# Expert biases: one row per quadrant of partitions and a VectorE shuffle in place of a broadcasting transfer

## The reference, cut to what matters

```python
    def expert_block(args):
        e, x_b = args
        gu = x_b @ w_gu[e] + b_gu[e]
        gate = jnp.minimum(gu[..., ::2], SWIGLU_LIMIT)
        up = jnp.clip(gu[..., 1::2], -SWIGLU_LIMIT, SWIGLU_LIMIT)
        return ((up + 1.0) * (gate * jax.nn.sigmoid(SWIGLU_ALPHA * gate))) @ w_dn[e] + b_dn[e]
```

## Time and profile before

| what | value |
|---|---|
| median of 3 runs | 3250.05 us (3247.81 to 3250.87) |
| the profiled execution's own time | 3250.61 us |
| its span, first to last instruction | 3248.8 us |
| mean granted TensorE clock | 0.910 of full speed |
| loop of 47 turns, about | from 1314 to 2548 us of the span |
| bytes moved by DMA | 569.55 MB |
| expert weight transfers called, skipped ones included | 576, of 1024 KB |
| bias transfers called, skipped ones included | 96, of 256 KB |

### The profile page before, as it was taken

The page is one execution under the profiler, slowest core; times in us unless marked ns, Lnnn a source line. Parts: engine busy times, 40 slices in busy tenths (PEclk is TensorE's granted clock), DMA queues, the critical chain, the costliest instruction groups (busy, mean ns, idle before and its releaser), DMA issues. The chain is left out here.

```text
span 3248.8 us, 51694 instructions
## 1 busy us (share of the span) xinstructions
PE 2634.1 (81%) x19262; PEld 1295.7 (40%) x19262; DVE 966.2 (30%) x2193; ACT 758.9 (23%) x1718; POOL 364.4 (11%) x339
## 2 busy tenths in 40 slices
PE   6778686856789993889888988898889589778999
PEld 2445363635464442323332323333333244355444
DVE  1263636363246425111111111111111321354012
ACT  2123332333050002222221212222222211254100
POOL 0030302130060000000000000000000200144000
PEclk8888787877899996899999999999999789887999
DMA  5100000000317314699999999499969612001112
GB/s 196 54 25 22 6 22 6 22 2 3 115 47 278 120 52 185 259 400 368 364 369 383 363 401 365 163 368 400 373 265 370 240 67 78 28 1 53 52 52 78
DMA packets 118951, 569.55 MB, mean 175 GB/s; under 512 B 13809, under 2 KB 17393, under 8 KB 67217
## 3 DMA queue, kind: packets, MB, share of 16 engines
q1 hardware_dynamic: 97184, 510.21, 40.2%
q10 hardware_dynamic: 15472, 36.16, 3.5%
q0 software_dynamic: 6144, 20.98, 1.8%
HBM read 760.50 MB, written 16.52 MB: 239 GB/s over the span
## 5 line engine op out<-in xcount | busy, mean ns | idle before, releaser
L1350 PE MATMUL moe_gu_ps<-expert_w,xgT 128*64 128x512 f32 x3008 | 683.1, 597 | 92.6 <-PEq L1315 92.6
L1350 PEld LDWEIGHTS moe_gu_ps<-expert_w,xgT 128*64 128x64 f32 x3008 | 245.4, 137 | 522.1 <-issue 522.1
L1376 PE MATMUL moe_down_ps<-expert_w,actT 128*64 128x512 f32 x1504 | 347.2, 598 | 67.4 <-PEq L1315 67.4
L1435 DVE TENSOR_TENSOR biased<-moe_gu_ps,b_gu 128x512 f32<-128x512 f32 x94 | 65.0, 692 | 936.9 <-DVEq L1315 936.9
L1376 PEld LDWEIGHTS moe_down_ps<-expert_w,actT 128*64 128x64 f32 x1504 | 114.4, 136 | 239.8 <-issue 239.8
L1397 ACT ACT_TABLE_LOAD x47 | 60.3, 1283 | 425.3 <-ACTq L1315 425.3
L1856 PE MATMUL ahead_ps<-hT,x 128*128 128x256 f32 (+1 forms) x288 | 127.6, 541 | 23.6 <-PEq L57 23.6
L1330 POOL COPY tokens<-token_of 128x1 uint32 x47 | 8.5, 182 | 1126.6 <-POOLq L1315 1126.6
L1279 ACT ACTIVATE xgT<-moe_xg_ps,ffn_shift,ffn_gain 128x64 f32<-128x64 f32 x384 | 119.0, 424 | 42.2 <-PE moe_xg_ps L1273 42.2
L1401 ACT COPY actT<-moe_act_ps 128x256 f32<-128x256 f32 x94 | 35.0, 372 | 399.9 <-ACTq L1315 399.9
L386 PE MATMUL b2p_ps<-b_w,b_hT 128*128 128x512 f32 (+1 forms) x320 | 119.4, 535 | 1.8 <-PEq L57 1.8
(11 more groups left out here) (684 smaller groups left out, 3685.0 us busy)
## 6 DMA issues: line engine op xcount, KB each, us to landing
expert_w<-in_w_experts SPq DMA_DIRECT2D x576, 1024.0 KB
late_w<-in_w_late SPq DMA_DIRECT2D x12, 2048.0 KB, 8.5
b_gu<-in_b_experts ACTq DMA_DIRECT2D x96, 256.0 KB
b_w<-in_w_in SPq DMA_DIRECT2D x10, 2048.0 KB, 7.6
ada_w<-in_w_ada SPq DMA_DIRECT2D x6, 2048.0 KB, 13.0
slot_rows<-yb ACTq DMA_DIRECT2D x94, 128.0 KB, 6.1
mix_w<-in_w_in_tok SPq DMA_DIRECT2D x5, 2048.0 KB, 9.9
x<-in_w_rkv SPq DMA_DIRECT2D x5, 1536.0 KB, 7.3
```

The lines of the kernel that those rows point to most:

```text
L1350: last = nc.tensor.matmul(ps_gu[SLOTS * j:SLOTS * j + SLOTS, half, :], xgT[:, k, :], w[:, i, at:at + 512], start=(k == 0), stop=(k == KD - 1),
L1376: last = nc.tensor.matmul(ps_dn[SLOTS * j:SLOTS * j + SLOTS, :], actT[:, half, q, SLOTS * a:SLOTS * a + SLOTS], w[:, i, at:at + 512], star ...
L1435: step(nc.vector.tensor_tensor(biased[:, :], ps_gu[:, half, :], b_gu[:, half, :], ALU.add))
```

## The change

A second buffer `b_rows` (128 partitions x 1024) is set to zero once. Each of the two bias transfers now writes one row of 4 KB into only two partitions (0 and 32 for row 0, 64 and 96 for row 1), the first partition of each group of 32. At the head of every turn VectorE waits for the bias, copies `b_rows` to `b_gu` with a shuffle in which all 32 partitions of a group take the group's first, and frees `b_rows`. The wait and the signal that stood in the two halves are gone.

```diff
+        b_rows = sb("b_rows", [P, D])
...
         def load_bias(act, expert, **when):
             for j in range(2):
-                act.dma_start(b_gu[SLOTS * j:SLOTS * j + SLOTS].rearrange("p h n -> p (h n)"),
-                              d["b_experts"][expert, j].unsqueeze(0).to_broadcast([SLOTS, D]), **when) \
+                act.dma_start(b_rows[SLOTS * j:SLOTS * j + SLOTS:32, :],
+                              d["b_experts"][expert, j].unsqueeze(0).to_broadcast([2, D]), **when) \
                     .then_inc(bias_here, 16)
...
+                nc.vector.memset(b_rows[:, :], 0.0).then_inc(s["rows_set"], 1)
...
             def _(act):
+                act.wait_ge(s["rows_set"], 1)
                 load_bias(act, 0)
...
                 with dve.Fori(0, turns):
+                    takes(dve, bias_here, 32)
+                    step(nc.vector.stream_shuffle(b_gu[:, :, :].rearrange("p h n -> p (h n)"), b_rows[:, :], [0] * 32))
+                    nc.vector.sem_inc(s["bias_free"], 1)
                     for half in range(2):
                         takes(dve, s["gu_made"])
-                        if half == 0:
-                            takes(dve, bias_here, 32)
                         step(nc.vector.tensor_tensor(biased[:, :], ps_gu[:, half, :], b_gu[:, half, :], ALU.add))
                         nc.vector.sem_inc(gu_read, 1)
-                        if half == 1:
-                            nc.vector.sem_inc(s["bias_free"], 1)
```

More of the change, by code:

```diff
@@ L1283, in modulate @@
             last.then_inc(xgT_made, 1)
-        with stage(nc, "moe_start", "tokens", "xg_turned", "set", pool_dma=(gathered,)) as (s, block):
+        with stage(nc, "moe_start", "tokens", "xg_turned", "set", "rows_set", pool_dma=(gathered,)) as (s, block):
             @block.vector
```

## The result

The changed kernel takes 3159.43 us in the median of 4 runs (3156.38 to 3165.14), against 3250.46 for the kernel before beside it. The ratio is 0.9718, with a 95% interval from 0.9697 to 0.9740: 91 us faster.

A forecast was written before the change was run, and what follows sets the result against it. The prediction took weight transfers in stretched groups of the expert loop's turns as the bound. 29 loads x 2.35 us = 68 us off 3250.6, other parts costing nothing, gave 3182 us, range 3168 to 3203.

The forecast's parts named there:

- eleven groups of turns: In the expert loop: 4 groups of three turns and 7 of four, where transfers run without pause; 29 loads inside.
- Saved per load: 2.78 - 0.43 = 2.35 us: In the expert loop: old bias transfer's cost less the new one's, counted for 29 loads, 68 us.
- What the new transfer costs: Per load in the expert loop: four 4 KB packets, two on the engine waited for, 0.43 us; bounds 0 and 0.86.
- long groups: Expert loop: 7 groups of four turns with two one-block experts, 108.79 us each, 15.2 above four unstalled turns; three loads each.
- What the old one costs: Per load in the expert loop: weights missing from five 6 us windows, 1.19 MB, 2.78 us (2.67 to 2.90).
- Short groups: Expert loop: 4 groups of three turns, two loads each; saving 4.7 of 5.3 us of stretch, so not cut off.
- the gather before the loop: Before the loop: shares engines with 0.52 MB less, could gain up to 1 us; left out of the sum.
- Price by bytes: In the expert loop, neighbours' slowing has another cause (mixing queues) and stays: only 35 us saved, 3215 us; chance 0.08.
- Two loaded engines: In the expert loop, many pieces fall on one or two engines, chunks wait: 17 or 114 us slower; chance 0.03.
- 13 packets' worth on one engine: Expert loop: the load on one engine, 2.78 / 0.21, from which the new transfer would make the kernel slower.
- The shuffle waits: VectorE's shuffle: rows landing over 13.4 us plus about 3 after the call; at 20 us, 112 slower; chance 0.02.
- the other signs: Loop: 2.5 MB weights per 6 us; groups 71 and 102 us; PE waits 60 us less; ScalarE queue 16 MB lighter.

The follow-up runs named there:

- kernel 3: Changed kernel without bias transfers in the loop, every expert given the first expert's bias, shuffle kept: 3159.47 us, 46 turns in 1121.93 us.
- experiment 12: Changed kernel with 16 KB instead of 4 KB for each of the four partitions, still two calls a turn: 3224.20 us, 46 turns in 1182.56 us.
- experiment 2: Changed kernel without the shuffle, VectorE adding b_rows itself, wait and signal where they were before the change: 3163.86 us.
- experiment 11: The changed kernel again, unaltered: 3161.09 us, 46 turns in 1126.01 us.
- kernel 9: Changed kernel with the shuffle made seven times in a row in each turn: 3160.92 us, 46 turns in 1125.18 us.
- kernel 1: Changed kernel with each bias transfer again covering all 64 partitions of b_rows, shuffle and earlier signal kept: 3247.72 us, ratio to before 1.0001.
- kernel 4: Kernel before, each partition reading its own 4 KB from the expert's weights instead of 64 partitions reading one row: 3249.54 us, ratio 1.0010.
- kernel 5: Kernel before, each of the two bias transfers writing every second of all 128 partitions instead of a block of 64: 3196.39 us, ratio 0.9832.
- kernel 6: Kernel before, one transfer over all 128 partitions read from the expert's weights, instead of two over 64 each: 3199.93 us, ratio 0.9864.
- experiment 10: Changed kernel with the shuffle made fourteen times in a row in each turn: 3468.16 us, 46 turns in 1422.03 us.
- kernel 8: Changed kernel with each two-partition transfer made four times, to four different sets of partitions: 3223.35 us, 46 turns in 1187.22 us.

## Why the prediction was wrong in size

The mechanism was right at every step: the loop is bound by transfers in eleven groups of turns, the loads of the bias lie on the path there, the stretched groups are where they were counted, and the shuffle costs nothing. The step that failed is the sum's term "Saved per load: 2.78 - 0.43 = 2.35 us". Measured are 3.10 and 0.16, so 2.94 us. This makes the turns give 83.2 us where 68.2 were summed, and it has used up the range by itself, whose lower end stands for 82. That the time fell 9 us below that end is mostly due to what lies outside the turns, for which the range left no room.

- *What the new transfer costs.* Taken 0.43 us, between 0 and 0.86; measured 0.16 (kernel 3). The four packets don't hold a chunk up by the whole time of two. On the 21 loads of the long groups this is 5.7 us of the miss.
- *What the old one costs.* Taken 2.78 us from what was missing in windows of 6 us; by the turn time 3.10, 0.3 more, 6.6 us in all. A window is not quite the whole transfer (157 of 160 packets in the earlier trace rows, 146 in the earlier trace rows): over the 59 us of this kernel shown with experiment 12 the stream loses 2.9 us per load, not 2.78. The other 0.2 us are open. The bounds of 2.67 and 2.90 were the spread of the windows, not of the price, and the range inherited this.
- *Short groups.* With 2.94 us saved per load they are cut off at their stretch: their last turns fell from 28.66, 28.99, 28.48 and 28.86 to 23.36 us, 21.6 in place of the 18.8 summed; 2.8 us of the miss. Together they are the 15 us by which the turns gave more.
- *Outside the turns.* 8.3 us of the difference of the two spans: 6.8 ahead of the router's mark, within its scatter, and 1.5 of small pieces, among them the gather before the loop, 1.2 us faster, which was left out at up to 1. In experiments 2, 3, 9 and 11 the kernels with this loop or less lie 83 to 88 us below the kernel before that ran beside them (3159 to 3164 against 3246 and 3249). So of the 91 us some are luck, and all of these medians are still below the range. Median less turn time is 2034 to 2036 us for the changed kernel and kernel 9, and 2038 to 2042 for kernels 1, 4, 5 and 6 with the full transfers, but also for kernels 2, 3 and 12 with small ones or none; so a gain outside the turns is not shown.
- *Price by bytes* (first rival) fell with all windows and with kernel 1. Its cause, "mixing of two queues", is refuted as the reason for the extra cost too: the same queue costs 1.36 us once the partitions are spread (kernel 5). Bytes over rate nearly hold there, 1.22 against 1.36, but not for a transfer into one half of the partitions. The Trainium skill's section cited for that rule (Anatomy of one DMA) speaks of transfers that GpSimd calls, and these are ScalarE's.
- *Two loaded engines* (rival on the slow side): kernel 12, which pays 2.25 us for 64 KB, shows chunks that wait for a late part, whether by two engines or by few partitions. With 16 KB it is 0.16 us. My condition, 13 packets' worth on one engine, was not reached.
- *The shuffle waits*: the threshold was said to be 13.4 us plus about 3 for the landing, and experiments 9 and 10 bear it out; it landed after 6.3. The shuffle was done 7.1 us ahead of its add, not the "more than 8" given as a sign; the other signs came out nearly as given.
- *Why the transfer was dear* I had left open, and my first guess after the result (the repeated row) was wrong.

## What to carry to other kernels

Where large transfers run without a pause and matmuls wait for each chunk, price a small transfer by what its neighbours lose while it passes, not by its bytes; here 0.52 MB cost 3.1 us of the stream in place of 1.2. A transfer into a block of 64 partitions is the dear kind here, a broadcast or not: spread over all 128 partitions it cost less than half, and one row per 32 partitions with a shuffle on an idle engine next to nothing. Before adding to a queue, find what stands behind it: ScalarE's calls had 3.4 us of cover, VectorE had room for six more shuffles, 9 us. A range needs room for the scatter of the rest of the program, not only for the terms of the sum.

## What the runs showed of the hardware that was not expected

- The same 128 packets of 4 KB cost the weights' stream 3.10 us when each transfer fills partitions 0 to 63 or 64 to 127, and 1.36 when each fills every second one. That the ports are the cause is the Trainium skill's rule ("SBUF — State Buffer", Door 1), which has the right sign; the runs show only the dependence on the partitions.
- 64 KB into four partitions held up the turns by 2.25 us a load while the weights' stream lost only 0.4 us of its bytes (kernel 12); 0.52 MB into halves of the partitions cost the stream itself 2.9 of the 3.1 us.
- After a wait of 2 to 3 us TensorE's matmuls were slower for a while, in most cases but not in all. The window from 1385 to 1390.4 us of kernel 8, behind its wait of 2.85 us, has a mean granted clock of 0.68, a mixture of the levels of 1.2 and 2.4 GHz; the one before it has 1.00, the upper level (third number from the right):

```profile
1378.00:1385.00 7.00, 4.02 (x18) 1.47 (x18) 1.34 (x4) 1.05 (x4) 0.00 (x0) 1.00 1.01 427
1385.00:1390.40 5.40, 5.36 (x18) 2.11 (x20) 0.32 (x2) 2.12 (x8) 1.16 (x2) 0.68 1.02 423
```

  Behind the wait of 2.81 us that ends at 1412.12 the clock stays at 1.00:

```profile
1412.00:1416.00 4.00, 3.88 (x18) 1.61 (x20) 0.00 (x0) 2.20 (x8) 1.16 (x2) 1.00 1.03 423
```

  The slow kind adds 1.7 us to the wait's own, in 25 of the 31 turns with a load. In the changed kernel, whose longest wait in front of down matmuls is 0.8 us, the turns stay at 1.00 in both windows shown above.
- Two calls of a transfer into 2 partitions keep ScalarE's queue 1.85 us, two into 64 partitions 1.33 us.
